# A decoder layer on eight cores: merged tiles kept in SBUF, output projection before cross-attention, FFN by seven products, down projection in two passes

## The reference

```python
def token_mixer(n, positions, w_in, ...):
    proj = n @ w_in                                   # 2048 x 9216: u, v, q, k, v_att, g_a, g_b
    y_a = chunked_spatial_gating(gelu(u), layer_norm(gelu(v)), ...) @ w_branch_a
    y_b = moba_attention(rope(q), rope(k), v_att) @ w_branch_b
    merged = sigmoid(g_a) * y_a + sigmoid(g_b) * y_b
    return merged @ w_tm_out                          # 2048 x 2048
def cross_attention(n, mem_n, w_q, w_kv, w_out):      # 4 heads of 128, 256 memory tokens
    s = einsum('bshd,bmhd->bhsm', n @ w_q, k) * 128 ** -0.5
    return einsum('bhsm,bmhd->bshd', softmax(s), v) @ w_out
def swiglu(n, w_gate, w_up, w_down):                  # hidden 5632
    return (silu(n @ w_gate) * (n @ w_up)) @ w_down
```

## Time and profile before

| | us |
|---|---|
| median of 3 runs | 3823.85 |
| lowest, highest run | 3820.01, 4373.37 |
| the profiled execution | 3819.3 |
| its span (slowest core, core 0) | 3817.7 |
| spans of all cores | 3799.3 to 3817.7 |
| output projection and cross-attention begin | 1466 |
| FFN matmuls end | 3121 |

### The profile page before, as it was taken

One profiled execution on the slowest core, in us unless ns is written; L12 is line 12 of the kernel. 1 busy time (PEld: TensorE's weight loads), 2 busy tenths in 40 slices (PEclk: granted clock), 3 DMA queues, 4 the chain that ended last, 5 costly groups with the idle time before them and its releaser, 6 DMA issues.

```text
span 3817.7 us, 53509 instructions; the slowest of 8 cores (3799.3 to 3817.7 us)
## 1 busy us (share of the span) xinstructions
PE 3558.9 (93%) x18426; PEld 1710.9 (45%) x18538; DVE 1263.7 (33%) x2223; ACT 1008.2 (26%) x1917; POOL 435.6 (11%) x523
## 2 busy tenths in 40 slices
PE   5999999999788998999699999999999989996998
PEld 3444444444455443555444444444444434442443
DVE  4763564222477555677421011110011100000333
ACT  5533323334577201666410000000000000000111
POOL 1100000000000000111121222121212110000000
PEclk9999999999999998999899999999999999998999
DMA  9135566664822477666864765454444538768554
GB/s 191 70 45 84 103 111 112 111 105 89 160 60 75 94 231 188 201 208 215 212 93 56 91 83 61 56 60 56 57 60 52 63 66 220 193 199 194 214 214 167
DMA packets 409817, 469.64 MB, mean 123 GB/s; under 512 B 211920, under 2 KB 354512, under 8 KB 388048
## 3 DMA queue, kind: packets, MB, share of 16 engines
q0 software_dynamic: 308416, 180.38, 33.5%
q1 hardware_dynamic: 101136, 285.84, 22.7%
...
## 4 chain that ended last, share of the span: by engine, by line
PE 81%; DMA 9%; DVE 5%; issue 3%; ACT 1%; SPq 0%; POOL 0%; DVEq 0%; ACTq 0%; POOLq 0%
PE ps L316 80%; DMA RA<-HIDT 2%; DMA sgb<-GS 2%; DVE acc L342 2%; PE ps L319 1%; DMA wv<-w_in 1%; DMA RB<-w_fd 1%; DMA N<-wslot 1%; DMA MG<-ma 1%; DMA memx<-mem 0%; SPq L358 0%; DMA GS<-stgh 0%; DVE acc L332 0%; DMA H<-RA 0%; DMA VD<-stg 0%
## 5 line engine op out<-in xcount | busy, mean ns | idle before, releaser
L316 PE MATMUL ps<-RB,wslot 128*128 128x512 bf16 x3712 | 805.7, 379 | 0.8 <-DVE RB L332 0.6
L316 PEld LDWEIGHTS ps<-RB,wslot 128*128 128x128 bf16 x3712 | 363.0, 98 | 438.4 <-issue 2.2
L332 DVE TENSOR_TENSOR xt<-xt,ps 128x512 bf16<-128x512 f32 x176 | 121.1, 688 | 1064.1 <-PE ps L316 1064.0
L316 PE MATMUL ps<-RB,gtab 128*128 128x512 bf16 x1920 | 417.7, 379 | 0.0
L329 ACT ACTIVATE xt<-ps 128x512 f32<-128x512 f32 x176 | 105.1, 597 | 1082.0 <-PE ps L316 1082.0
L316 PEld LDWEIGHTS ps<-RB,gtab 128*128 128x128 bf16 x1920 | 187.9, 98 | 226.5
L316 PE MATMUL ps<-n1op,ws1r 128*128 128x512 f16 x1024 | 234.7, 382 | 9.8 <-ACT pf L349 9.8
L316 PE MATMUL ps<-n1op,ws0r 128*128 128x512 f16 x1024 | 234.1, 381 | 3.8 <-ACT pf L349 3.8
L316 PE MATMUL ps<-RA 128*128 128x512 bf16 (+1 forms) x1201 | 218.7, 338 | 19.6 <-DMA RA<-HIDT 18.8
L316 PE MATMUL ps<-RBH,mT 128*128 128x512 f16 x1024 | 234.7, 381 | 2.2 <-DVE tmp L332 2.2
L358 POOL DMA_DIRECT2D HIDT<-xt x176 | 135.3, 768 | 776.2 <-DVE xt L332 776.2
...
## 6 DMA issues: line engine op xcount, KB each, us to landing
RA<-HIDT SPq DMA_DIRECT2D x24, 1408.0 KB, 7.0
RB<-HIDT SPq DMA_DIRECT2D x24, 1408.0 KB, 6.8
H<-RA SPq DMA_DIRECT2D x32, 1024.0 KB, 5.2
xt<-H SPq DMA_DIRECT2D x32, 1024.0 KB, 8.3
HIDT<-xt POOLq DMA_DIRECT2D x176, 128.0 KB, 2.8
ws0r<-w_in POOLq DMA_DIRECT2D x16, 1024.0 KB, 13.0
ws1r<-w_in POOLq DMA_DIRECT2D x16, 1024.0 KB, 12.8
...
```

The source lines that it names most:

```text
L316: self.S.add("pe", lambda e: e.matmul(out, lhsT, rhs, start=start, stop=stop, **kw), reads, writes)
L332: self.S.add(eng, lambda e: e.tensor_tensor(out, in0, in1, op), reads, writes)
```

## The change

- MG and N3 go. A reads its tiles from `ma` in SBUF (`f_a`), all 16 tiles one after another. Its evacuation is a Square on ScalarE and, on VectorE, the product with the gain table into the row buffer; the residual is added by one instruction (`f_add`), and the normalised tile is written by ScalarE (`f_nn`). The transposed tile goes back into the place of its merged tile in `ma` (`f_c`).
- Cross-attention reads n from `ma`. `w_co` is cast in HBM during the input projection (WOH, four more casts on POOL's queue) and loaded by SP after A's last matmul, when RBH's place is free; there is one buffer `no` for normalised tiles. n3 goes from PSUM straight into eight FFN operands (A11 to A22 for two token halves).
- The gain of the FFN's norm is multiplied into the weights (`fgain`). 20 blocks of 256 hidden columns take the quads of the input projection for both token halves; two blocks take 256 plain matmuls for the first token half inside the cross-attention planner, at priority 9000. There are 84 quads. `fprep` (gain and sums of one slot) is hooked into the middle of quads of the second token half. 44 casts of 128 rows of `w_fd` to WDH (f16, HBM) stand on POOL's queue between them. HIDT is f16 and stored from SP.
- Down projection: `units` runs column block 0 for tiles 0 to 3, block 1 for the same, both together for tiles 4 to 11, one after the other for 12 to 15, then blocks 2 and 3 for all 16: 40 HIDT loads where 48 were. The columns are f16 loads from WDH on POOL's queue into three places, W0, W1, W2. Y3 and the output are stored from SP; the last tile is finished in four pieces.

```diff
+    casts = [(WBH, w_b, r, bWBH[r]) for r in range(8)] + [(WTH, w_tm, r, bWTH[r]) for r in range(16)] + [(WOH, w_co, r, bWOH[r]) for r in range(4)]
-        if 2 <= bi < 26:
+        if 2 <= bi < 30:
...
-                B.dma("sp", MG[tt], ma[:, tt * 2048:(tt + 1) * 2048], dmg, bma[tg], [bMG[tt]])
...
-            B.act(junk[:, q * 512:(q + 1) * 512], p[:], AF.Square, [pb], [bjk[q], sb_], accum=s_[:, cb:cb + 1])
-            B.act(ap[:, cb * 512:(cb + 1) * 512], p[:], AF.Identity, [pb], bufs)
+            B.act(junk, p[:], AF.Square, [pb], [bjk, sb_], accum=s_[:, cb:cb + 1])
...
+            B.tt(ap[:, cb * 512:(cb + 1) * 512], p[:], gt[:, cb * 512:(cb + 1) * 512], ALU.mult, [pb, bg], bufs)
...
-            B.stt(y, y, s_[:, 6:7], gt[:], ALU.mult, ALU.mult, yb + [sb_, bg], yb)
-            B.tt(y, y, x_, ALU.add, yb + xb, yb)
+            B.stt(y, y, s_[:, 6:7], x_, ALU.mult, ALU.add, yb + xb + [sb_], yb)
...
-            B.ts(n, y, s_[:, 10:11], None, ALU.mult, None, yb + [sb_], nb_)
+            B.act(n, y, AF.Identity, yb + [sb_], nb_, scale=s_[:, 10:11])
...
-                        B.mm(p[:], m_[:, kc * 128:(kc + 1) * 128], RBH[:, kc * 2048 + cb * 512: kc * 2048 + (cb + 1) * 512],
+                        B.mm(p[:], ma4[:, tt, kc, :], RBH[:, kc * 2048 + cb * 512: kc * 2048 + (cb + 1) * 512],
...
+    own = T("sp", 0.0, f_own, Aend, 0, lat=0.0)
+    give(NO, "no0", [(no_r[:], [no_r.b], no_r.d)], [own], lambda: None)
...
+    lo = [T("sp", 0.8, f_wo(ch), [own], -7 + ch, lat=8.0) for ch in range(2)]
+    lgo = T("sp", 0.6, lambda: B.dma("sp", gto[:], gains[1:2, :].partition_broadcast(128), gto.d, [], [gto.b]), lo, 0, lat=5.0)
...
-                    B.tt(o, p[:].bitcast(BF16).rearrange("p (k t) -> p k t", k=8), g_, ALU.mult, [pb, bconst], wb)
+                    B.cp(f_.t[:, :, c4 * 128:(c4 + 1) * 128], p[:].bitcast(F16).rearrange("p (k t) -> p k t", k=8), [pb], [f_.b[c4]])
...
+    def fgain(sl):
+        for kc in range(KC):
+            w_ = sl.raw[:, kc, :]
+            bb = sl.bq[kc // 8]
+            B.ts(w_, w_, gcols[:, 3, kc:kc + 1], None, ALU.mult, None, bb + [bconst], bb)
...
+    quads = [(0, 0, 1), (0, 1, 1), (1, 0, 1), (1, 1, 1)]
+    for b in range(2, NBF - 2):
+        quads += [(b, w, p) for p in range(2) for w in range(2)]
+    quads += [(b, w, p) for p in range(2) for b in (NBF - 2, NBF - 1) for w in range(2)]
...
+    def fprep(i):
+        fgain(fw[i])
+        fw[i].sums()
+    for qi, (b, w, p) in enumerate(quads):
...
+        if p == 1 and 0 < b < NBF - 2:
+            mid[4] = lambda b=b, w=w: fprep((2 * b + 2 + w) % 4)
...
+        if w == 1 and p == 1 and b + 2 < NBF:
+            fw_load(b + 2)
+        if (qi % 2 or qi % 16 == 8) and wdr[0] < HC:
+            wd_cast(wdr[0])
...
+        if (b, w, p) == (NBF - 1, 1, 0):
+            pre_down()
...
+    W1.load(1)
...
+    units = [((0,), t) for t in range(4)] + [((1,), t) for t in range(4)] + [((0, 1), t) for t in range(4, 12)]
+    units += [((0,), t) for t in range(12, 16)] + [((1,), t) for t in range(12, 16)]
...
+    units += [((2, 3), t) for t in range(NT)]
+    for ui, (cols, t) in enumerate(units):
+        h_ = nxt
+        if ui + 1 < len(units):
+            nxt = load_hT(units[ui + 1][1])
+        if ui == 2:
+            W2.load(2)
```

More of the change, by code:

```diff
@@ L544, in _program @@
     dcon2 = B.dsem("const2")
-    dgain = [B.dsem("gain%d" % i) for i in range(2)]
     psum = [B.st.enter_context(nc.psum_tensor("ps%d" % i, [128, 512], F32)) for i in range(8)]
@@ L1943, in _program @@
             ex.append(T("act", 0.62, f_e, [sc], pg, rel=[(BS, sk_)]))
+        qall[g] = qs[-1:]
         for c in range(2):
@@ new lines, in hid_store @@
+    def hid_store(blk, tg, ap, b, d):
+        B.dma("sp", HIDT[tg * 4:(tg + 1) * 4, :, blk * 256:(blk + 1) * 256].rearrange("c p n -> p c n"),
+              ap.rearrange("p (c n) -> p c n", c=4), d, [b], [bHID[blk][tg]])
+    P.run()
+    FOP[(S1, 0)].claim()
+    FOP[(S2, 0)].claim()
+    FOP[(S4, 0)].claim()
+    FOP[(S1, 1)].claim()
+    FOP[(S2, 1)].claim()
+    FOP[(S4, 1)].claim()
+    fslots[2].claim()
+    fslots[3].claim()
+    NBF = HID // 256
+    fw = [fslots[i] for i in range(4)]
@@ new lines, in fw_load, with fsum @@
+    def fw_load(b):
+        fw[(2 * b) % 4].load(w_fg, b * 256)
+        fw[(2 * b + 1) % 4].load(w_fu, b * 256)
+    fw_load(1)
+    pf = rot("fpf", [188416 + i * 2048 for i in range(8)], 512, F32)
+    fsr = rot("ffs_", [114688 + i * 2048 for i in range(4)], 512, F32)
+    for_ = rot("ffo_", [112640, 61440, 63488], 1024, F16)
+    ysum = {"S1": (S1, A21, A22, ALU.add), "S2": (S2, S1, A11, ALU.subtract),
+            "S3": (S3, A11, A21, ALU.subtract), "S4": (S4, A12, S2, ALU.subtract)}
+    def fsum(p, which):
+        o, a_, b_, op = ysum[which]
+        O, A_, B_ = FOP[(o, p)], FOP[(a_, p)], FOP[(b_, p)]
+        for kh in range(2):
+            ks = slice(kh * 4, kh * 4 + 4)
+            B.tt(O.t[:, ks, :], A_.t[:, ks, :], B_.t[:, ks, :], op, A_.b + B_.b, O.b)
@@ new lines, in prod, with h_gate, done, add @@
+    def prod(pb_, a, w, p, start, ops):
+        pt_, pb = pb_
+        wv_, wb_ = ops[w]
+        f_ = FOP[(a, p)]
+        for k in range(8):
+            B.mm(pt_[:], wv_[:, k, :], f_.t[:, k, :], start and k == 0, k == 7, [wb_] + f_.b, [pb], skip_group_check=True)
+        tick()
+    fsv = {}
+    def h_gate(p):
+        def done(i, l, ap, b):
+            t_, b_, _ = fsr.next()
+            B.act(t_[:], ap, AF.Silu, [b], [b_])
+            fsv[(i, l)] = (t_, b_)
+        def add(i, l, bank, s):
+            t_, b_ = s
+            B.tt(t_[:], bank[0][:], t_[:], ALU.add, [bank[1], b_], [b_])
+            return lambda: done(i, l, t_[:], b_)
+        def direct(i, l, bank):
+            done(i, l, bank[0][:], bank[1])
+        return add, direct
@@ new lines, in load_hT, with pre_down @@
+        B.dma("sp", h_[:], HIDT[tt], h_.d, [bHID[b][tt // 4] for b in range(NBF)], [h_.b])
+        return h_
+    pre = {}
+    def pre_down():
+        W0.claim()
+        W0.load(0)
+        hts[0].claim()
+        pre[0] = load_hT(0)
+    quads = [(0, 0, 1), (0, 1, 1), (1, 0, 1), (1, 1, 1)]
+    for b in range(2, NBF - 2):
+        quads += [(b, w, p) for p in range(2) for w in range(2)]
+    quads += [(b, w, p) for p in range(2) for b in (NBF - 2, NBF - 1) for w in range(2)]
+    for w_ in ("S1", "S2", "S3", "S4"):
+        fsum(1, w_)
```

683 lines of the change are left out of this document (337 added, 346 removed).

## The result

The changed kernel takes 3665.27 us (median of 3 runs, 3662.99 to 3665.78) against 3823.85: a ratio of 0.9589, 95% interval 0.9561 to 0.9616. It is faster, as forecast, but 70 us slower than forecast, and 0.27 us above the upper end of the range, [3545, 3665]. The profiled execution took 3665.27 us, its span is 3663.7 (core 3).

A forecast was written before the change was run, and what follows sets the result against it. TensorE, busy 3558.9 of 3817.7 us, was taken as the bound. 3819.3 - 145.1 + 12 - 4 - 35 - 57 = 3590.2, plus 4.5 for the median: 3595 us, range [3545, 3665].

The forecast's parts named there:

- Fewer FFN matmuls: FFN: 4960 matmuls in place of 5632, at 0.2159 us each; -145.1 us.
- Weight preparation: FFN quads: gain multiplied into weight slots and four sums on VectorE, mostly hidden; +12 us, bounds +2 and +40.
- 6 us on the first four: First four FFN quads: sums of the activations and two preparations fall together, costing 6 us.
- Rival B: FFN: preparation exposed, 10.2 us not 8.4, all 40 prepared half-blocks wait 1.8 us; 72 in place of 6; chance 0.13.
- yb stage: Stage of 123.0 us for 512 matmuls: 16 stores of merged tiles leave its DMA queues; -4 us, bounds 0 and -8.
- Output projection and cross-attention: From 1466.0 us to the FFN: 55 us idle or slow beyond 383.5 of work falls to 20; -35, bounds -53 and -10.
- I put 10: Cross-attention: 10 us left idle, as three evenly filled engines cannot all be hidden, though FFN matmuls fill from the eighth tile.
- Rival A: Cross-attention paced by its one buffer of normalised tiles, up to 11.7 us a tile against 9.3; 38 us more; chance 0.17.
- Down projection: Last stage, 697.0 us before: 608 of matmuls, 23 waiting, 9.5 tail, so 640.5; -57, bounds -45 and -68.
- rival C: Down projection: weight columns W1 and W3 late, a column taking 43 us; 37 us late, total 3632; chance 0.12.
- The stores' landing, 2.8 before: Down projection: second HIDT load waits 2.8 us for hidden-row stores, lands 12.1 after issue, so 5.5 us late.
- Rival E: FFN: weight slots land late, later than 43 us, each block lasting longer; at 60 us the sum is 3935; chance 0.05.

The follow-up runs named there:

- e3: Changed kernel without the FFN gain multiplied into the weights of blocks 1 to 21; first four quads 55.9 us, other eighty 966.9.
- e9: Changed kernel with five edits: early second HIDT tile, later W2, last pieces' own semaphores, preparation in portions, cross-attention gain in fours with 30 us slot landing; ratio 0.9433.
- e7: Changed kernel with each slot's gain multiplications in five portions between a quad's products, sums in a sixth; other eighty quads 969.0 us against 983.6.
- e12: e9 with second-half sums in the cross-attention plan, block 1's preparations in portions, first-half sums after later quads; first four quads 48.8 us, other eighty 977.7; ratio 0.9436.
- e11: Changed kernel with the 16 stores of merged tiles back on SP; A begins at 1454 us against 1453 and takes 254.0 against 240.5.
- e8: Changed kernel, planner told slots land after 30 us, each slot's gain cut into four tasks in cross-attention; that stage 227.8 us against 245.8.
- e10: e9 with second-half sums in the cross-attention plan, first-half sums on GpSimd, cross-attention's gain row before w_co; first four quads 75.7 us, cross-attention 265.4.

## Why the prediction was right or wrong

By its own terms, on the profiled cores, us:

| part | forecast | measured | error |
|---|---|---|---|
| to A's first matmul | -4 | -11.2 | -7 |
| A and cross-attention without the filler (438.7, now 435.1) | -35 | -3.6 | +31 |
| FFN with the filler (1215.9, now 1109.8) | -145.1 + 12 = -133.1 | -106.1 | +27 |
| down projection (697.0, now 663.9) | -57 | -33.1 | +24 |

The errors add to 75 us, which is the miss of the sum, 3590.2 against 3665.3.

- *Fewer FFN matmuls: right.* Eighty quads without a hindrance take 966.9 to 967.3 us, 12.09 each (e3, e9).
- *Weight preparation: mechanism right, size wrong.* It was put at 12 and cost 39 (70.9 + 983.6 - 84 x 12.09), the upper bound. One preparation was well priced, 8.4 against 6.0 + 3.2. "0.3 us on 20 gate quads" should have been the 16 that the other eighty lost: 18 waits of up to 1.6 us and slower matmuls behind them. There the place in one piece was nearly the whole price (e7). And "6 us on the first four" was 22: there stand four preparations, two of them in one quad, and sixteen sums of 1.2 us, which I had only named, not added up. There VectorE is filled, and a change of place alone only moves the loss on (e12). Rival B, 72, had the mechanism.
- *yb stage: right in sign, outside its bounds (0 to -8).* 123.0 became 111.0, without idle time. The step "16 stores leave its DMA queues" named the wrong cause: with the stores back A begins no later (e11). What went with them, the loads of `mT` and two gain rows among the gate loads, fits the rows (before, VectorE waited 44.7 us for gates in this stage, now 11.9). So 7 us of the sum were won by something that the prediction did not have.
- *Output projection and cross-attention: wrong, and the largest error.* A runs without idle time, as forecast, and the wait of the earlier trace rows, 40.8 of the 51 us idle there, is gone. But 435.1 is 51.6 us over the 383.5 of the work, where 20 had been left: 40 idle, the rest matmuls at the lower clock (granted 0.93), which the sum had nowhere. Some 6 were at the hand-over (8 forecast); so "I put 10" became some 45. The step "VectorE ... near 8.8" a tile had the tile's own work right, but left out the gain of four slots, 24 us in all, and the waits for two slots, 3.3 and 5.3 us; the bound of -10 had none of it. Cutting up the gain and telling the planner when the slots land won 18 of it without leaving out any work (e8). Rival A fell: TensorE waited 2.1 us for `no`.
- *Down projection: half right.* Columns from f16 come in time, rival C fell (no wait for `wd`); later HIDT waits came to 6.8 us where I had 10. The 4.3 us of a HIDT tile in the sum for W1, "78 ns of 16 engines x 55", stands in no row; nothing came to hang on it. Two steps failed. "The stores' landing, 2.8 before" was 15.7 beside two weight columns, and the tile 17 us later than forecast. "The tail ... 9.5" was 19.1, because four pieces on one semaphore are a chain; it is longer than with the one piece of before, 15.9. Some 6 us more are matmuls at the lower clock (granted 0.95).
- *Rival E fell:* slots landed after 9.4 to 12.5 us in the quads (medians of the four slots). The lock of VectorE and GpSimd was seen at another place (e10).
- *The range.* It let two bad ends meet; here three did, and two of them, cross-attention and the down projection, lay outside their own bounds. That the time came out only 0.27 us beyond the range is no merit of the sum: the range was wide, and the unforeseen 7 us of the yb stage helped.

The Trainium skill's formula for one DMA ("DMA: Bandwidth & Descriptors", section "Anatomy of one DMA — SWDGE (gpsimd) path") gives two columns 2.0 us + 11.5 MB / 436 GB/s, some 28 us, as an estimate. The trace again does not agree: the last piece of the second column landed 42.8 us after its own issue, with the rest of both columns and HIDT tiles beside it. (The HIDT tile that the prediction held against the formula came on SP's queue, while the section is on GpSimd's.)
